# Bank alternation in the up projection and a 512 + 32 column split in the output projection of a decoder layer on one NeuronCore

## The chip, the cores and the metric

The kernel runs on one core of one Trainium2 chip. The metric is the device time of that core in microseconds. Before the change the median of two runs is 2403.22 us (2402.18 and 2404.27).

## The reference

One decoder layer serves a prompt of 512 tokens and 32 sample tokens (8 sequences with 4 new tokens each), all in float32, with a model width of 2048, 16 query heads, 4 key and value heads of 128, and a hidden width of 8192:

```python
xp, xs = rms_norm(hp, attn_norm), rms_norm(hs, attn_norm)
qp, kp, vp = project_qkv(xp, w_qkv, q_norm, k_norm)       # the same for the sample tokens
lf = log_sigmoid(x @ w_fgate + b_fgate); c = cumsum(lf)   # forgetting gates
mix_p = fox_attention(qp, kp, vp, c_p, c_p, 0, 128)
mix_s = fox_attention(qs, k_all, v_all, ...)              # 1024 cached keys from pages, and 4 new
hp, hs = hp + mix_p @ w_o, hs + mix_s @ w_o
h = h + square(relu(rms_norm(h, mlp_norm) @ w_up)) @ w_down
```

The outputs are the new activations, keys, values and log forget values of both groups.

## The kernel before, in words

Activations lie with the model dimension on the partitions and the tokens along the row: T = 544 columns (512 of the prompt, then 32 sample tokens), in 16 slices of 128 rows. `xT` is the residual stream. `act_hi` and `act_lo` hold the input of the current projection, split into two float32r parts whose sum is the float32 value. Every weight is split in the same way, and a product is computed as three matmuls: w_hi times the low part, w_hi times the high part and w_lo times the high part.

The weights go through the kernel in 338 units of 8 x 128 x 128 values (512 KB). For every unit SyncE loads `w_raw` (four buffers), ScalarE casts it into `w_hi` (L628, two buffers), VectorE subtracts to make `w_lo` (L906, two buffers), and TensorE multiplies. `unit` (L1323) is this last step: after a wait for w_lo it goes through the unit's 8 chunks, and a chunk is six matmuls, since the 544 columns are taken as two halves of HALF = 272. The accumulator is two banks of PSUM, half 0 in the first and half 1 in the second, 272 columns used of each:

```python
def acc(slot, rows=P):
    return ps[0:rows, 2 * slot:2 * slot + 2, 0:HALF]
```

Within a chunk the order is: half 0 by L1332 and L1333 (the same bank twice), half 1 by L1332 and L1333 (the other bank twice), then L1336 for half 0 and for half 1. Every matmul brings a weight load of its own, also where the weights are the ones just used. Two accumulators (slots 0 and 1, banks 0 to 3) are used in turn. An output tile of the query, key, value, output and up projections is two units (16 chunks, the whole model dimension); one of the down projection is one unit, and it is added to `xT` for each of 8 blocks of the hidden width.

The stages follow each other on TensorE: transposes of the input, gates, values, keys and queries (50 units, `model_tile`), the prompt's attention, the sample tokens' attention, the output projection (32 units, 16 tiles, `model_tile`), and 8 blocks of the MLP, each with 16 units of up projection (`up_tiles`) and 16 of down projection (`down_tiles`), the last with the transposes of the output among them.

Around the output projection: VectorE adds each tile's accumulator to `xT` (L1236) and frees the slot (`acc_free`), ScalarE squares the row (L834) and GpSimd adds the squares for the next norm. Around an up tile: VectorE takes the accumulator through relu and the norm's factor (L1260), ScalarE squares it and makes `u_hi`, VectorE makes `u_lo`. The order of everything is written out by hand in one program for each engine, with semaphores between them. TensorE's waits in these stages are for w_lo, for a free slot, and at a stage's first tile for the chunks of its input.

Of the kernel before, what the change touches and what calls it, by code (L numbers as in the profile page):

```python
# [31 lines left out]
ALU = mybir.AluOpType  # L32
# [6 lines left out]
def fox_layer(nc, x_prompt, x_sample, cache_k, cache_v, cache_logf, page_table, attn_norm, w_qkv, q_norm,  # L39
              k_norm, w_fgate, b_fgate, w_o, mlp_norm, w_up, w_down,  # L40
              y_prompt, y_sample, nk_prompt, nv_prompt, nf_prompt, nk_sample, nv_sample, nf_sample):
    _, SEQ, D = x_prompt.shape
    NB, DS, _ = x_sample.shape
    _, NPOOL, PAGE, NKV, HD = cache_k.shape
    NH = cache_logf.shape[3]
    NPG = page_table.shape[1]
# [3 lines left out]
    T = SEQ + NS  # L50
    HALF = T // 2
# [3 lines left out]
    UC = 8  # L55
# [11 lines left out]
    with ExitStack() as ctx:  # L67
        def sem(name):
            return ctx.enter_context(nc.semaphore(name))
# [5 lines left out]
        def at(name, shape, dt, offset=None):  # L75
            n = 4
            for s in shape[1:]:
                n *= s
            if offset is None:
                offset = top[0]  # L80
                top[0] += -(-n // 64) * 64
            return nc.alloc_sbuf_tensor_at(name, shape, dt, offset=offset), offset, offset + n

        xT, _, _ = at("xT", [P, KC, T], F32)
        act_hi, act_at, _ = at("act_hi", [P, KC, T], F32R)
        act_lo, _, act_end = at("act_lo", [P, KC, T], F32R)
# [3 lines left out]
        w_hi, _, _ = at("w_hi", [P, 2, UC, P], F32R)  # L90
        w_lo, _, _ = at("w_lo", [P, 2, UC, P], F32R)
# [85 lines left out]
        psf = ps[:, :, :].rearrange("p b n -> p (b n)")  # L177
# [5 lines left out]
        def halves(ap):  # L183
            return ap.rearrange("p (a n) -> p a n", a=2)

        def acc(slot, rows=P):
            return ps[0:rows, 2 * slot:2 * slot + 2, 0:HALF]
# [20 lines left out]
        w_lo_made = sem("w_lo_made")  # L208
        unit_used = sem("unit_used")
        acc_free = [sem("acc_free0"), sem("acc_free1")]  # L210
# [63 lines left out]
        mix_lo = sem("mix_lo")  # L274
# [11 lines left out]
        BLK_U, BLK_T = 32, 24  # L286
# [615 lines left out]
        def _(dve):  # L902
# [306 lines left out]
            last = (NB // 2 - 1, 1)  # L1209
# [15 lines left out]
            def o_tile(i, k):  # L1225
                u, t = U_O + 2 * k, T_O + k
                split(i + (u + 2) // 4, (u + 2) % 4)
                split(i + (u + 3) // 4, (u + 3) % 4)
                o_add(i, k)

            def o_add(i, k):
                u, t = U_O + 2 * k, T_O + k
                dve.wait_ge(unit_used, 4 * i + u + 2)
                dst = xT[:, 2 * i + k, :] if isinstance(i, int) else \
                    xT[:, bass.ds(2 * i + k, 1), :].rearrange("p o t -> p (o t)")
                nc.vector.tensor_tensor(halves(dst), halves(dst), acc(t % 2), ALU.add).then_inc(acc_free[t % 2], 1)  # L1236

            o_tile(0, 0)
            o_tile(0, 1)
# [5 lines left out]
            for c in range(KC):  # L1245
                gained_lo(1, g_mlp, c)
                if c == 1:
                    o_add(KC // 2 - 1, 1)
                    split((U_M + 1) // 4, (U_M + 1) % 4)
# [52 lines left out]
        def _(pe):  # L1302
# [4 lines left out]
            for c in range(KC):  # L1307
# [4 lines left out]
                for t, (t0, n) in enumerate(token_tiles):  # L1312
                    o = 2048 + 1024 * (c % 2) + t0
                    ins = pe.transpose(psf[:, o:o + n], x_tok[0:n, t, c * P:(c + 1) * P], ident[0:n, 0:n])
                ins.then_inc(x_turned, 1)

            def column_sums(src, out, signal):

                for a in range(2):
                    ins = pe.matmul(out[:, a, :], ones[:], src[:, a * HALF:(a + 1) * HALF], start=True, stop=True)  # L1320
                ins.then_inc(signal, 1)

            def unit(i, k, out, hi, lo, first, last, chunk_waits=None):  # L1323

                pe.wait_ge(w_lo_made, 4 * i + k + 1)
                s = k % 2
                for c in range(UC):
                    if chunk_waits is not None:
                        chunk_waits(c)
                    for a in range(2):  # L1330
                        h, l = hi(c)[:, a * HALF:(a + 1) * HALF], lo(c)[:, a * HALF:(a + 1) * HALF]
                        pe.matmul(out[:, a, :], w_hi[:, s, c, :], l, start=first and c == 0, stop=False)  # L1332
                        pe.matmul(out[:, a, :], w_hi[:, s, c, :], h, start=False, stop=False)  # L1333
                    for a in range(2):
                        h = hi(c)[:, a * HALF:(a + 1) * HALF]
                        ins = pe.matmul(out[:, a, :], w_lo[:, s, c, :], h, start=False, stop=last and c == UC - 1)  # L1336
                ins.then_inc(unit_used, 1)
                return ins

            def model_tile(i, u, t, waits=None, between=None, wait_acc=True):  # L1340

                if wait_acc:
                    pe.wait_ge(acc_free[t % 2], i + t // 2)
                out = acc(t % 2)
                for half in range(2):
                    uu = u + half
                    unit(i + uu // 4, uu % 4, out, lambda c: act_hi[:, half * UC + c, :],
                         lambda c: act_lo[:, half * UC + c, :], half == 0, half == 1,
                         None if waits is None else (lambda c: waits(half * UC + c)))
                    if half == 0 and between is not None:  # L1350
                        between()

            def norm_waits(n):
                def waits(c):
                    pe.wait_ge(act_lo_made, KC * n + c + 1)
                return waits


            model_tile(0, 0, 0, waits=norm_waits(0), wait_acc=False)
            pe.wait_ge(sq_added, KC - 1)  # L1360
            column_sums(tmp_c[:, 0, :], acc(2), ssq_ready)
# [12 lines left out]
            for i in range(NKV // 2):  # L1374
                for k in range(2):
                    u, t = U_V + 2 * k, T_V + k
                    model_tile(i, u, t, wait_acc=not (i == 0 and k == 0), between=turn_gates if 2 * i + k == 1 else None)
# [13 lines left out]
            def kq_tile(i, k, u0, t0, m0):  # L1391
                u, t, m = u0 + 2 * k, t0 + k, m0 + k
                first = isinstance(i, int) and m + 2 * i == 0
                model_tile(i, u, t, between=None if first else (lambda: head_sums(i, m - 1)))
# [9 lines left out]
            for b in range(NB):  # L1404
                ins = pe.matmul(psf[:, 3072 + b * PAGE:3072 + (b + 1) * PAGE],
                                lf_page[:, b * NPG:(b + 1) * NPG, :].rearrange("p n h -> p (n h)"), tri[:],
                                start=True, stop=True)
# [172 lines left out]
            last = (NB // 2 - 1, 1)  # L1580
# [5 lines left out]

            for k in range(2):
                u, t = U_O + 2 * k, T_O + k
                model_tile(0, u, t, waits=(lambda c: pe.wait_ge(mix_lo, c + 1)) if k == 0 else None)
            with pe.Fori(1, KC // 2) as i:  # L1590
                for k in range(2):
                    u, t = U_O + 2 * k, T_O + k
                    model_tile(i, u, t)

            def up_tiles(j, i, waits=None):
                for k in range(2):
                    u, t = U_M + 2 * k, T_M + k
                    pe.wait_ge(acc_free[t % 2], j * (BLK_T // 2) + i + t // 2)
                    for half in range(2):
                        uu = u + half  # L1600
                        unit(j * (BLK_U // 4) + i + uu // 4, uu % 4, acc(t % 2),
                             lambda c: act_hi[:, half * UC + c, :], lambda c: act_lo[:, half * UC + c, :],
                             half == 0, half == 1,
                             None if waits is None or k else (lambda c: waits(half * UC + c)))
                        if waits is not None and k == 0 and half == 0:
                            pe.wait_ge(sq_added, 2 * (KC - 1))
                            column_sums(tmp_c[:, 0, :], acc(2), ssq_ready)
# [69 lines left out]
```

## Time and profile before

| what | value |
|---|---|
| median of the runs | 2403.22 us |
| the runs | 2402.18 and 2404.27 us |
| span of the profiled execution, from its first to its last instruction | 2395.7 us |
| TensorE busy in matmuls | 2289.5 us, 96% |
| VectorE, ScalarE, GpSimd busy | 945.3, 668.9, 164.8 us |
| mean granted TensorE clock | 0.986 |
| output projection, its first matmul to its last | 629.6 to 825.0 us of the span |
| matmuls in it | 1536 |
| units of up projection in the 8 MLP blocks | 128 (6144 matmuls) |

The page gives no time for the profiled execution besides its span. The faster of the two runs is 6.5 us longer than the span, the median 7.5 us: what lies around the program's instructions. A matmul's duration in the rows includes the way through the array and overlaps the next matmul, so the rate of a stretch is read from the distance between starts, or from the number of matmuls in a window without idle time.

### The profile page before, as it was taken

The page shows a single profiled execution, that of the slowest core. Times are in us where ns is not written, and L with a number is a line of the kernel's source. Part 1 is how long each engine was busy: PE and PEld are TensorE (multiplying, and loading weights), DVE is VectorE, ACT ScalarE, POOL GpSimd, SP SyncE. Part 2 cuts the span into 40 slices and gives each one's busy share as a digit, 9 for nine tenths or more (in the row PEclk, how much of TensorE's full clock was granted, in tenths as well). Part 3 has the DMA queues.
Part 4 walks back from the last instruction along what each step waited for, and adds up shares of the span by engine and source line. Part 5 has one row for each costly group of instructions (what it writes and reads, how often), then busy time and mean ns, then how long its engine had stood idle before and what let it go on. Part 6 is the DMA issues. An engine that isn't in the chain of part 4 may idle for free.

```text
span 2395.7 us, 44612 instructions
## 1 busy us (share of the span) xinstructions
PE 2289.5 (96%) x18061; PEld 2212.0 (92%) x18061; DVE 945.3 (39%) x1188; ACT 668.9 (28%) x938; POOL 164.8 (7%) x245
## 2 busy tenths in 40 slices
PE   6999996777899999999999999999999999999998
PEld 5999994545799999999999999999999999999998
DVE  6366668944422443333333323323333333333332
ACT  4233336632322332122122112212212212212212
POOL 5400002233011100000000000000000000000000
PEclk9999998989899999999999999999999999999999
DMA  4333222179333233332323233333322233333333
GB/s 131 87 90 88 84 75 72 35 230 300 113 88 88 79 88 89 88 88 85 87 85 87 86 88 88 88 88 88 87 85 86 85 87 87 88 88 88 88 88 92
DMA packets 392889, 229.27 MB, mean 96 GB/s; under 512 B 18736, under 2 KB 372528, under 8 KB 392832
## 3 DMA queue, kind: packets, MB, share of 16 engines
q1 hardware_dynamic: 385376, 216.91, 31.1%
q0 software_dynamic: 7456, 11.55, 1.6%
q8 instruction: 42, 0.69, 0.1%
q14 instruction: 15, 0.12, 0.0%
HBM read 221.14 MB, written 7.28 MB: 95 GB/s over the span
## 4 chain that ended last, share of the span: by engine, by line
PE 87%; DVE 4%; DMA 2%; ACT 2%; issue 2%; SPq 2%; POOL 1%; ACTq 0%; DVEq 0%; POOLq 0%
PE ps L1333 28%; PE ps L1332 28%; PE ps L1336 28%; DMA k_high<-in_cache_k 2%; DVE probs L1074 1%; PE ps L1542 1%; POOL tmp_c L525 1%; DVE probs L1076 1%; ACT w_hi L628 1%; DVE nmax L1080 0%; ACT probs L720 0%; PE ps L1465 0%; PE ps L1504 0%; PE ps L1440 0%; SPq L410 0%
## 5 line engine op out<-in xcount | busy, mean ns | idle before, releaser
L1332 PE MATMUL ps<-act_lo,w_hi 128*128 128x272 f32 x3360 | 910.7, 289 | 7.8 <-DVE act_lo L917 3.9
L1333 PE MATMUL ps<-act_hi,w_hi 128*128 128x272 f32 x3360 | 909.6, 290 | 0.0
L906 DVE TENSOR_TENSOR w_lo<-w_raw,w_hi 128x1024 fp32r<-128x1024 f32 x338 | 415.3, 1229 | 1177.7 <-ACT w_hi L628 1177.5
L628 ACT CAST w_hi<-w_raw 128x1024 fp32r<-128x1024 f32 x338 | 354.3, 1048 | 1333.0 <-PE ps L1336 1333.0
L1336 PE MATMUL ps<-act_hi,w_lo 128*128 128x272 f32 x3360 | 698.5, 289 | 0.0
L1332 PEld LDWEIGHTS ps<-act_lo,w_hi 128*128 128x128 f32 x3360 | 634.8, 189 | 8.9 <-issue 4.1
L1333 PEld LDWEIGHTS ps<-act_hi,w_hi 128*128 128x128 f32 x3360 | 636.2, 189 | 0.1
L1332 PE MATMUL ps<-u_lo,w_hi 128*128 128x272 f32 x2048 | 554.4, 289 | 1.1
L1333 PE MATMUL ps<-u_hi,w_hi 128*128 128x272 f32 x2048 | 553.2, 289 | 0.0
L1336 PEld LDWEIGHTS ps<-act_hi,w_lo 128*128 128x128 f32 x3360 | 527.4, 189 | 0.0
L1336 PE MATMUL ps<-u_hi,w_lo 128*128 128x272 f32 x2048 | 425.0, 289 | 0.0
L1332 PEld LDWEIGHTS ps<-u_lo,w_hi 128*128 128x128 f32 x2048 | 385.8, 188 | 2.8 <-DVE u_lo L1264 2.8
L1333 PEld LDWEIGHTS ps<-u_hi,w_hi 128*128 128x128 f32 x2048 | 386.4, 189 | 0.0
L1336 PEld LDWEIGHTS ps<-u_hi,w_lo 128*128 128x128 f32 x2048 | 320.5, 188 | 0.0
L1284 DVE TENSOR_TENSOR xT<-xT,ps 128x544 f32 (+1 forms) x128 | 91.3, 713 | 13.2 <-PE ps L1336 13.2
L1264 DVE TENSOR_TENSOR u_lo<-tmp_b,u_hi 128x544 f32 (+1 forms) x64 | 46.4, 726 | 104.4 <-ACT u_hi L864 104.4
L862 ACT ACTIVATE tmp_b<-tmp_a 128x544 f32<-128x544 f32 x64 | 42.1, 658 | 126.8 <-DVE tmp_a L1260 126.8
L1017 DVE RECIPROCAL tmp_c<-tmp_c 128x544 f32<-128x544 f32 x20 | 70.9, 3546 | 0.8 <-ACT tmp_c L676 0.8
L525 POOL TENSOR_TENSOR tmp_c<-tmp_c,tmp_b 128x544 f32<-128x544 f32 x30 | 45.0, 1499 | 209.8 <-ACT tmp_b L834 207.4
L1454 PEld LDWEIGHTS ps<-ident,probs 128*128 128x128 f32 x160 | 19.8, 154 | 40.9 <-DVE probs L1089 28.0
L1454 PE MATMUL ps<-ident,probs 128*128 128x128 f32 x160 | 23.6, 302 | 29.7 <-DVE pT L1098 26.9
L729 ACT ACTIVATE probs<-probs,nmax 128x128 f32<-128x128 f32 (+1 forms) x64 | 36.0, 569 | 41.8 <-DVE nmax L1080 41.7
(163 smaller groups left out, 1147.5 us busy)
## 6 DMA issues: line engine op xcount, KB each, us to landing
w_raw<-in_w_up SPq DMA_DIRECT2D x128, 512.0 KB, 4.0
w_raw<-in_w_down SPq DMA_DIRECT2D x128, 512.0 KB, 3.9
w_raw<-in_w_qkv SPq DMA_DIRECT2D x48, 512.0 KB, 3.7
w_raw<-in_w_o SPq DMA_DIRECT2D x32, 512.0 KB, 3.9
k_low<-in_cache_k SPq DMA_DIRECT2D x32, 256.0 KB, 4.4
k_high<-in_cache_k SPq DMA_DIRECT2D x32, 256.0 KB, 5.2
v_page<-in_cache_v SPq DMA_DIRECT2D x32, 256.0 KB, 6.3
v_page<-in_cache_v POOLq DMA_DIRECT2D x32, 256.0 KB, 6.0
```

Source lines behind the costliest of these rows:

```text
L525: nc.gpsimd.tensor_tensor(tmp_c[:, 0, :], tmp_c[:, 0, :], tmp_b[:, c % 2, :], ALU.add).then_inc(sq_added, 1)
L628: nc.scalar.copy(w_hi[:, k % 2], w_raw[:, k % 4]).then_inc(w_hi_made, 1)
L729: nc.scalar.activation(probs[:, k, t, 0:w], probs[:, k, t, 0:w], ACT.Exp, bias=nmax[:, k % 2, t:t + 1], accum_out=rsum[:, k % 2, t:t + 1]) ...
L862: nc.scalar.activation(tmp_b[:, k, :], tmp_a[:, k, :], ACT.Square).then_inc(relu_sq, 1)
L906: nc.vector.tensor_tensor(w_lo[:, k % 2], w_raw[:, k % 4], w_hi[:, k % 2], ALU.subtract).then_inc(w_lo_made, 1)
L1017: nc.vector.reciprocal(tmp_c[:, 0, :], tmp_c[:, 0, :]).then_inc(head_rec, 1)
L1264: nc.vector.tensor_tensor(sl(u_lo), tmp_b[:, k, :], sl(u_hi), ALU.subtract).then_inc(u_lo_made, 1)
L1284: nc.vector.tensor_tensor(halves(dst), halves(dst), acc(t % 2), ALU.add).then_inc(acc_free[t % 2], 1)
L1332: pe.matmul(out[:, a, :], w_hi[:, s, c, :], l, start=first and c == 0, stop=False)
L1333: pe.matmul(out[:, a, :], w_hi[:, s, c, :], h, start=False, stop=False)
L1336: ins = pe.matmul(out[:, a, :], w_lo[:, s, c, :], h, start=False, stop=last and c == UC - 1)
L1454: ins = pe.transpose(psf[:, o:o + P], probs[:, k, t, j * P:(j + 1) * P], ident[:])
```

## The change

In `up_tiles` the unit's matmuls are put in another order: low part for half 0 and half 1, high part for half 0 and half 1, then the w_lo product for both. The number and the size of the matmuls stay. In the output projection a new `mixer_tile` calls `unit_split`, which cuts the 544 columns at 512 instead of 272: three matmuls of 512 columns, then three of 32. The accumulator there is one run of 544 columns from the slot's first bank, so 512 lie in that bank and 32 in the next, and VectorE's addition reads it in one run. Waits and semaphore counts are the same.

```diff
@@ o_add @@
-                nc.vector.tensor_tensor(halves(dst), halves(dst), acc(t % 2), ALU.add).then_inc(acc_free[t % 2], 1)
+                nc.vector.tensor_tensor(dst, dst, psf[:, 1024 * (t % 2):1024 * (t % 2) + T], ALU.add
+                                        ).then_inc(acc_free[t % 2], 1)
@@ tensor @@
+            def unit_turns(i, k, out, hi, lo, first, last, chunk_waits=None):
+
+                pe.wait_ge(w_lo_made, 4 * i + k + 1)
+                s = k % 2
+                for c in range(UC):
+                    if chunk_waits is not None:
+                        chunk_waits(c)
+                    for a in range(2):
+                        pe.matmul(out[:, a, :], w_hi[:, s, c, :], lo(c)[:, a * HALF:(a + 1) * HALF],
+                                  start=first and c == 0, stop=False)
+                    for a in range(2):
+                        pe.matmul(out[:, a, :], w_hi[:, s, c, :], hi(c)[:, a * HALF:(a + 1) * HALF],
+                                  start=False, stop=False)
+                    for a in range(2):
+                        ins = pe.matmul(out[:, a, :], w_lo[:, s, c, :], hi(c)[:, a * HALF:(a + 1) * HALF],
+                                        start=False, stop=last and c == UC - 1)
+                ins.then_inc(unit_used, 1)
+                return ins
+
+            def unit_split(i, k, out, hi, lo, first, last, chunk_waits=None):
+
+                pe.wait_ge(w_lo_made, 4 * i + k + 1)
+                s = k % 2
+                for c in range(UC):
+                    if chunk_waits is not None:
+                        chunk_waits(c)
+                    for cols in (slice(0, SEQ), slice(SEQ, T)):
+                        pe.matmul(out[:, cols], w_hi[:, s, c, :], lo(c)[:, cols], start=first and c == 0, stop=False)
+                        pe.matmul(out[:, cols], w_hi[:, s, c, :], hi(c)[:, cols], start=False, stop=False)
+                        ins = pe.matmul(out[:, cols], w_lo[:, s, c, :], hi(c)[:, cols], start=False,
+                                        stop=last and c == UC - 1)
+                ins.then_inc(unit_used, 1)
+                return ins
@@ after model_tile @@
+            def mixer_tile(i, u, t, waits=None):
+
+                pe.wait_ge(acc_free[t % 2], i + t // 2)
+                for half in range(2):
+                    uu = u + half
+                    unit_split(i + uu // 4, uu % 4, psf[:, 1024 * (t % 2):1024 * (t % 2) + T],
+                               lambda c: act_hi[:, half * UC + c, :], lambda c: act_lo[:, half * UC + c, :],
+                               half == 0, half == 1, None if waits is None else (lambda c: waits(half * UC + c)))
@@ output projection @@
-                model_tile(0, u, t, waits=(lambda c: pe.wait_ge(mix_lo, c + 1)) if k == 0 else None)
+                mixer_tile(0, u, t, waits=(lambda c: pe.wait_ge(mix_lo, c + 1)) if k == 0 else None)
...
-                    model_tile(i, u, t)
+                    mixer_tile(i, u, t)
@@ up_tiles @@
-                        unit(j * (BLK_U // 4) + i + uu // 4, uu % 4, acc(t % 2),
+                        unit_turns(j * (BLK_U // 4) + i + uu // 4, uu % 4, acc(t % 2),
```

TensorE in the output projection, one chunk before (`act_lo` and `act_hi` are the split input, `w_hi` and `w_lo` the split weights, `ps` is PSUM):

```order
L1332 MATMUL ps<-act_lo,w_hi 128x272
L1333 MATMUL ps<-act_hi,w_hi 128x272
L1332 MATMUL ps<-act_lo,w_hi 128x272
L1333 MATMUL ps<-act_hi,w_hi 128x272
L1336 MATMUL ps<-act_hi,w_lo 128x272 x2
```

and the same chunk of the changed kernel:

```order
L1368 MATMUL ps<-act_lo,w_hi 128x512
L1369 MATMUL ps<-act_hi,w_hi 128x512
L1370 MATMUL ps<-act_hi,w_lo 128x512
L1368 MATMUL ps<-act_lo,w_hi 128x32
L1369 MATMUL ps<-act_hi,w_hi 128x32
L1370 MATMUL ps<-act_hi,w_lo 128x32
```

Six matmuls and six weight loads stand there as before, with 1632 columns in all as before; three of the matmuls are now longer and three short, and the short ones stand in a row.

TensorE in the up projection reads before as in the first fence (the same lines of `unit`). The chunk of the changed kernel there:

```order
L1349 MATMUL ps<-act_lo,w_hi 128x272 x2
L1352 MATMUL ps<-act_hi,w_hi 128x272 x2
L1355 MATMUL ps<-act_hi,w_lo 128x272 x2
```

Each x2 is half 0 and then half 1, so every matmul now goes to the other bank than the one ahead of it. On the other engines no instruction moves.

## Rows read from the trace of the kernel before

**Rows 1.** The page: TensorE's busy time, and its granted clock in 40 slices.

```profile
PE 2289.5 (96%) x18061; PEld 2212.0 (92%) x18061; DVE 945.3 (39%) x1188; ACT 668.9 (28%) x938; POOL 164.8 (7%) x245
...
PEclk9999998989899999999999999999999999999999
```

**Rows 2.** Busy time in two stretches: the output projection, and its steady part.

```profile
core 0: us, PE busy (x) PEld busy (x) DVE busy (x) ACT busy (x) POOL busy (x), PEclk, DMA share, GB/s
629.00:825.00 196.00, 195.38 (x1536) 195.19 (x1536) 57.46 (x62) 50.34 (x61) 18.98 (x14) 0.99 0.29 83
640.00:820.00 180.00, 180.00 (x1436) 180.00 (x1435) 45.59 (x45) 41.23 (x45) 18.98 (x14) 1.00 0.31 88
```

**Rows 3.** Groups by line, 640 to 820 us: busy, mean ns, idle and releaser.

```profile
L1333 PE MATMUL ps<-act_hi,w_hi 128*128 128x272 f32 x479 | 129.4, 290 | 0.0
...
L1332 PEld LDWEIGHTS ps<-act_lo,w_hi 128*128 128x128 f32 x478 | 90.0, 188 | 0.0
...
L906 DVE TENSOR_TENSOR w_lo<-w_raw,w_hi 128x1024 fp32r<-128x1024 f32 x30 | 36.8, 1225 | 130.8 <-ACT w_hi L628 130.8
L628 ACT CAST w_hi<-w_raw 128x1024 fp32r<-128x1024 f32 x30 | 31.5, 1049 | 108.4 <-PE ps L1336 108.4
...
L1236 DVE TENSOR_TENSOR xT<-xT,ps 128x544 f32 (+1 forms) x15 | 10.7, 713 | 0.0
```

**Rows 4.** Timeline of TensorE, 700.5 to 702.9 us: start, duration, instruction.

```profile
700.54 0.29 PE L1332 MATMUL ps<-act_lo,w_hi 128*128 128x272 f32 x1
700.67 0.29 PE L1333 MATMUL ps<-act_hi,w_hi 128*128 128x272 f32 x1
700.79 0.29 PE L1332 MATMUL ps<-act_lo,w_hi 128*128 128x272 f32 x1
700.92 0.29 PE L1333 MATMUL ps<-act_hi,w_hi 128*128 128x272 f32 x1
701.04 0.41 PE L1336 MATMUL ps<-act_hi,w_lo 128*128 128x272 f32 x2
701.29 0.29 PE L1332 MATMUL ps<-act_lo,w_hi 128*128 128x272 f32 x1
...
702.80 0.29 PE L1332 MATMUL ps<-act_lo,w_hi 128*128 128x272 f32 x1
```

**Rows 5.** The same view near the stage's start, at half clock.

```profile
632.48 0.43 PE L1332 MATMUL ps<-act_lo,w_hi 128*128 128x272 f32 x1
...
633.84 0.43 PE L1332 MATMUL ps<-act_lo,w_hi 128*128 128x272 f32 x1
```

**Rows 6.** Timeline around two 8-column matmuls, weight loads (PEld) among them.

```profile
206.19 0.31 PEld L1413 LDWEIGHTS ps<-c_pg,earlier 128*128 128x128 f32 x2
206.31 0.28 PE L1413 MATMUL ps<-c_pg,earlier 128*128 128x8 f32 x2
206.42 0.19 PEld L1332 LDWEIGHTS ps<-act_lo,w_hi 128*128 128x128 f32 x1
206.45 0.37 PE L1332 MATMUL ps<-act_lo,w_hi 128*128 128x272 f32 x1
206.53 0.19 PEld L1333 LDWEIGHTS ps<-act_hi,w_hi 128*128 128x128 f32 x1
206.66 0.29 PE L1333 MATMUL ps<-act_hi,w_hi 128*128 128x272 f32 x1
206.66 0.19 PEld L1332 LDWEIGHTS ps<-act_lo,w_hi 128*128 128x128 f32 x1
```

**Rows 7.** Timeline of TensorE around one head's product of probabilities and values.

```profile
490.82 2.32 PE L1465 MATMUL ps<-pT,v_st 128*128 128x512 f32 x8
492.98 0.71 PE L1454 MATMUL ps<-ident,probs 128*128 128x128 f32 x5
```

**Rows 8.** One line's instructions: counts, durations in ns, shapes.

```profile
L1465 PE MATMUL ps<-pT,v_st x128: 272/485/1062, 396.3 to 499.3; 128*128 128x512 f32 x32, 128*128 128x384 f32 x32, 128*128 128x256 f32 x32, 128*128 128x128 f32 x32
```

## The prediction

> **What bounds the kernel now.** I read the page first, for which engine is full. TensorE is busy for 2289.5 of 2395.7 us and no other engine passes 40% of the span [rows 1]. The clock line shows 9 (90% or more) outside three slices, so the columns run at 2.4 GHz nearly everywhere. Then the windows of the output projection, the stage of the larger edit: between 640 and 820 us TensorE is busy for 180.00 of 180 us with 1436 matmuls, at a granted clock of 1.00 [rows 2]. So there a matmul starts every 180/1436 = 0.1253 us, and nothing waits. The reader is to see beside it what the others do: in the same 180 us VectorE makes w_lo 30 times (36.8 us) and waits 130.8 us for ScalarE, ScalarE casts 30 times (31.5 us) and waits 108.4 us for TensorE, and the addition L1236 takes 10.7 us [rows 3]. The weights are ready early. Whatever a chunk of six matmuls costs on TensorE goes straight into the time, one for one.
>
> Third, the timeline, for the step between two starts. From 700.54 to 702.80 there are three chunks, 0.753 us each, 0.1256 us a matmul [rows 4]. At 2.4 GHz 272 columns take 0.1133 us, so 12 ns come on top. The same matmul at half clock, near the stage's start, shows no such excess: six take 633.84 - 632.48 = 1.36 us, 0.2267 each, which is 272 columns at 1.2 GHz and nothing more [rows 5]. So the 12 ns belong to something that doesn't halve with the clock, and the weight load that every matmul brings is the candidate.
>
> **What a weight load costs.** The trace has one place where the matmuls are too short to cover it. Two 8-column matmuls are followed by the next unit, and there the weight loads start at 206.42 and 206.53, 0.11 us apart, while one of them covers a matmul of 8 columns and the next waits behind it: the matmul of 206.45 is recorded with 0.37 us instead of 0.29, since it was issued and then held up for 0.08 us [rows 6]. The next load, 0.13 us later, runs beside 272 columns. So a load is hidden behind a matmul that lasts over 0.11 us, and where the matmul is shorter the load sets the step, at 0.11 to 0.13 us.
>
> The Trainium skill, page "TensorE: Matmul & The Clock Gate", section "LDWEIGHTS (loading the stationary operand)", says that a load takes its column count over 1.2 GHz, whatever the rows. For 128 columns that is an estimate of 107 ns from that page, and the trace agrees with its 0.11 us. The sum doesn't use it.
>
> **The output projection.** Its 1536 matmuls are 768 pairs. A pair is now 2 x 0.1253 = 0.2507 us. After the change a pair is one matmul of 512 columns and one of 32.
>
> - 512 columns at 2.4 GHz are 0.2133 us, long enough to cover the next load. What comes on top has no row, since no full-rate stream of that width is in the trace. From below: the plain float32 matmuls of L1465, which take two clocks a column and show as two records each, have eight records of 512, 512, 384, 384, 256, 256, 128 and 128 columns between 490.82 and 492.98 [rows 7, 8]. That is 2.16 us for 2560 columns, 2.133 us at two clocks each, so 3 ns a record: 0.216 us. From above: the excess grows with the columns as it stands at 272, 0.1256 x 512/272 = 0.236 us. With the 12 ns kept per matmul it is 0.226. I take 0.222, between the first and the last.
> - 32 columns are 13 ns of work, and the step is the load of the matmul behind it. A run of three short ones has three such steps (32 to 32 twice, then 32 to the next 512). From below 0.11 us, from above the 0.125 of now. I take 0.113, since the array's stream is nearly idle beside these loads, as it was at 206.42 [rows 6].
>
> A pair becomes 0.222 + 0.113 = 0.335 us, which is 0.084 more, and 768 pairs give +64.7 us. The ends: 0.216 + 0.11 = 0.326 gives +57.8; 0.236 + 0.125 = 0.361 gives +84.7. The stage grows from 195.4 to some 260 us.
>
> Nothing hides it. ScalarE and VectorE need 1.05 and 1.23 us for a unit that now takes 6.0 us and will take 8.0 [rows 3], and the final tile's addition is the same 0.71 us; read in one run over two banks instead of two, it carries the same 544 columns, and I cost it at nothing. Even 0.1 us on each of 16 additions would lie under the next tile but for the last. The next norm's squares, on GpSimd, get more time per tile, not less. The stage's first microseconds run at half clock [rows 5]; there a pair would go from 0.453 to 0.427 + 0.11 us, the same 0.084.
>
> **The up projection.** 128 units of 8 chunks, 6144 matmuls, whose count, columns and loads stay. The diff is in the banks: of the six steps of a chunk, two stay in a bank now (L1332 to L1333, twice) and four change it; afterwards all six change. So the trace of before shows the price of both. The steps within a bank read 0.13 and 0.13, those that change it 0.12, 0.12 and a mean of 0.125 over two [rows 4]; starts are given to 10 ns, and over three chunks all six have a mean of 0.1256. I see no difference, and with one of up to 5 ns either way on two steps of each of 1024 chunks the bound is -10 to +10 us. I take 0. What the alternation would relieve, a matmul that waits for the one ahead to leave its bank, would have shown in these two steps.
>
> **The sum.** 2395.7 + 64.7 + 0 = 2460.4 us of span. The median of the runs stands 7.5 us above the span of before (2403.2 against 2395.7), so 2468 us, 2.7% more. A difference under about 2% (48 us) can't be told from none by a measurement of this kernel: the bounds of slower lie at 2451.
>
> **The rivals.**
>
> *The short matmuls cost next to nothing (7%).* If the load of a matmul could run ahead by more than one, three short ones would be covered by the 512-column ones, which leave 0.1 us of the load path free each. For it: the two 8-column matmuls are recorded within 0.28 us, the second 28 ns behind the first [rows 6]. Against: the loads themselves keep their 0.11 us, and the matmul behind is held up. A pair would be 0.222 + 0.028 = 0.250, the change 768 x 0 = 0, and the time 2403, not slower. It decides as soon as a short matmul takes less than 0.09 us (then the total is under 2%).
> The skill's page "TensorE: Matmul & The Clock Gate", section "Wait — 56ns, not 53.3ns?", speaks for this one: it gives N/2.4 plus 2.5 ns for a warm matmul and a floor of about 25 ns for small ones, 216 + 25 = 241 ns for the pair by that page, an estimate of 2396 us. It is a rule for matmuls without loads of their own, and rows 6 show the load.
>
> *The alternation does pay (5%).* If the 12 ns were a collision in PSUM that only a full alternation avoids, the 6144 matmuls would fall to 0.1133 + 0.003 = 0.1163 us, 9 ns each, -57 us, and the total would be 2468 - 57 = 2411: no change. Against: four of six steps alternate already and are no faster [rows 4].
>
> *A narrow matmul in this format runs as two records (5%),* as the plain float32 ones do [rows 8], with two loads each: 0.222 + 0.226 = 0.448 a pair, +151 us, 2555.
>
> *The clock drops in the output projection (3%).* The array streams 544 columns, 227 ns, in 335 ns instead of in 251, and the page shows 8 tenths in slices of the attention [rows 1]. At half clock throughout a pair is 0.427 + 0.11, +220 us, 2623; a tenth of the stage so costs some 20 us more.
>
> **How the numbers follow.** The forecast as worked out has 80%: 2468, with an own range from 2403.2 + 57.8 - 10 = 2451 to 2403.2 + 84.7 + 10 = 2498. The ends of both terms together are unlikely, and the rivals lie on both sides of it, so the range is 2450 to 2496. Slower by over 2% holds 76 of the 80, with the two dear rivals 84%. Within 2%: 4 of the forecast, and most of the first two rivals, 14%. Faster by over 2% needs both of these together, 2%.
>
> **What would show it.** In the output projection's timeline of the changed kernel the three 512-column starts should lie 0.216 to 0.236 us apart and the three short ones 0.11 to 0.125; the window of that stage should hold the same 1536 matmuls in about 260 us with no idle time and a clock of 1.00. In the up projection the mean step should still read 0.125 or 0.126, and a block of the MLP should take the same time. The forecast is wrong if the short steps read under 0.09, if the wide ones show another excess than 3 to 23 ns, if the up projection's step moves by over 2 ns, or if TensorE idles in the output projection for something else.

## The result, and the profile after

The changed kernel takes 2473.97 us (median of 2 runs, 2473.61 and 2474.32) against 2403.22 us: 1.0307 times as long, with a 95% interval of 1.0285 to 1.0329. The forecast was 2468 us, in a range from 2450 to 2496.

The span went from 2395.7 to 2472.7 us, 77.0 more. By the page of the changed kernel TensorE alone is busy for longer, 2362.1 us instead of 2289.5, while the other engines' work is the same to 0.3 us. These lines answer to [rows 1]:

```profile
PE 2362.1 (96%) x18061; PEld 2249.3 (91%) x18061; DVE 945.6 (38%) x1188; ACT 668.7 (27%) x938; POOL 164.8 (7%) x245
...
PEclk9999998988899999999999999999999999999999
```

The windows of the output projection, as in [rows 2], over the whole stage and its steady part:

```profile
core 0: us, PE busy (x) PEld busy (x) DVE busy (x) ACT busy (x) POOL busy (x), PEclk, DMA share, GB/s
637.00:904.00 267.00, 266.46 (x1536) 232.56 (x1536) 57.02 (x62) 50.19 (x61) 18.91 (x14) 0.99 0.21 61
650.00:900.00 250.00, 250.00 (x1458) 218.39 (x1458) 46.82 (x46) 41.32 (x45) 18.91 (x14) 1.00 0.22 64
```

The same 1536 matmuls fill 266.5 us instead of 195.4, without idle time, and at full clock but for the first 5.7 us. In the steady part that is 2 x 250/1458 = 0.343 us a pair, against 0.251.

One chunk and a little more in the timeline of weight loads (PEld) and matmuls; the columns are start, duration and instruction:

```profile
699.84 0.40 PE L1369 MATMUL ps<-act_hi,w_hi 128*128 128x512 f32 x1
699.84 0.19 PEld L1370 LDWEIGHTS ps<-act_hi,w_lo 128*128 128x128 f32 x1
700.07 0.39 PE L1370 MATMUL ps<-act_hi,w_lo 128*128 128x512 f32 x1
700.07 0.19 PEld L1368 LDWEIGHTS ps<-act_lo,w_hi 128*128 128x128 f32 x1
...
700.30 0.18 PE L1368 MATMUL ps<-act_lo,w_hi 128*128 128x32 f32 x1
700.30 0.19 PEld L1369 LDWEIGHTS ps<-act_hi,w_hi 128*128 128x128 f32 x1
700.33 0.26 PE L1369 MATMUL ps<-act_hi,w_hi 128*128 128x32 f32 x1
700.41 0.19 PEld L1370 LDWEIGHTS ps<-act_hi,w_lo 128*128 128x128 f32 x1
700.44 0.26 PE L1370 MATMUL ps<-act_hi,w_lo 128*128 128x32 f32 x1
700.52 0.19 PEld L1368 LDWEIGHTS ps<-act_lo,w_hi 128*128 128x128 f32 x1
700.55 0.48 PE L1368 MATMUL ps<-act_lo,w_hi 128*128 128x512 f32 x1
700.63 0.19 PEld L1369 LDWEIGHTS ps<-act_hi,w_hi 128*128 128x128 f32 x1
700.87 0.40 PE L1369 MATMUL ps<-act_hi,w_hi 128*128 128x512 f32 x1
```

Two things are to be read here. From the first short matmul on, the loads start at 700.30, 700.41, 700.52 and 700.63: 0.11 us each, one behind the other. They set the pace and the array waits. And the matmuls' own starts mislead in this place. The second short one starts 0.03 us behind the first, but has 0.26 us instead of 0.18; the wide one at 700.55 has 0.48 instead of 0.40, and its successor comes 0.32 us later. A start is the moment at which a matmul was let go, and the 0.08 us on top of its duration are its wait for the weights. Add them, and the steps are 0.23, 0.11, 0.11, 0.11. It is the pattern of the 8-column matmuls in [rows 6].

At half clock, in the stage's first microseconds, the timeline of TensorE reads:

```profile
637.17 0.77 PE L1368 MATMUL ps<-act_lo,w_hi 128*128 128x512 f32 x1 [1.85 <-DVE act_lo L1221]
...
639.08 0.77 PE L1368 MATMUL ps<-act_lo,w_hi 128*128 128x512 f32 x1
639.65 0.63 PE L1369 MATMUL ps<-act_hi,w_hi 128*128 128x512 f32 x1
640.08 0.63 PE L1370 MATMUL ps<-act_hi,w_lo 128*128 128x512 f32 x1
...
641.00 0.77 PE L1368 MATMUL ps<-act_lo,w_hi 128*128 128x512 f32 x1
```

A chunk takes 1.92 us: three times 0.427 for the wide ones, and 0.213 for each short one. So the load takes twice as long at half the clock.

For the up projection the chain that ended last gives a mark once a block, ScalarE's cast of the same unit. First the kernel before, then the changed one:

```profile
1894.09 1.06 ACT w_hi L628
...
2087.34 1.06 ACT w_hi L628
...
2280.59 1.06 ACT w_hi L628
```

```profile
1391.89 1.06 ACT w_hi L628
...
1584.94 1.06 ACT w_hi L628
...
1777.99 1.06 ACT w_hi L628
```

A block takes 193.25 us before and 193.05 after. Now and then a block has 0.4 or 0.8 us more than that (one of the seven between these marks before, three of the seven after), in both kernels; such blocks are left out of the comparison. The new order gives 0.2 us for 16 units of 48 matmuls, which is 0.27 ns a matmul, and 1.6 us for the 128 units.

The stage's 71.1 us less these 1.6 leave 7.5 of the 77.0 us, and they lie ahead of the output projection. Its first matmul starts at 637.17 us, where the kernel before has it at 629.62 us. No edit stands there. The stage before it waits for pages of the cache (TensorE's waits for `k_high` sum to 19.2 us before and 24.8 after), and its length varies from run to run: in the kernels below the first matmul comes between 629.98 and 635.36 us. It is the reason too why the medians differ by 70.8 us and these two spans by 77.0. The profiled execution of the kernel before was a short one: in each later run the time is 1.6 us above the run's own span (2474.32 and 2472.7 us here), so that execution took some 2397 us and is neither of the two timed ones. The 6.5 and 7.5 us that the table of before puts down to what lies around the instructions are for the most part this difference between executions.

### The profile page after: what moved, and what is told of

It is laid out like the page before. It is cut to its first block, busy times and chain, and to the rows that moved or that the text cites. A ratio compares the mean times of both kernels' runs of the same rounds, so it can differ in the third digit from the quotient of the medians.

```text
span 2472.7 us, 44612 instructions
## 1 busy us (share of the span) xinstructions
PE 2362.1 (96%) x18061; PEld 2249.3 (91%) x18061; DVE 945.6 (38%) x1188; ACT 668.7 (27%) x938; POOL 164.8 (7%) x245
## 4 chain that ended last, share of the span: by engine, by line
PE 88%; DVE 3%; SPq 2%; DMA 2%; ACT 2%; issue 2%; POOL 1%; ACTq 0%; DVEq 0%; POOLq 0%
PE ps L1333 14%; PE ps L1334 14%; PE ps L1337 14%; PE ps L1355 10%; PE ps L1349 10%; PE ps L1352 10%; PE ps L1368 4%; PE ps L1369 4%; PE ps L1370 4%; DMA k_high<-in_cache_k 2%; PE ps L1509 1%; PE ps L1586 1%; DVE probs L1074 1%; POOL tmp_c L525 1%; SPq L410 1%
## 5 line engine op out<-in xcount | busy, mean ns | idle before, releaser
L1349 PE MATMUL ps<-act_lo,w_hi 128*128 128x272 f32 x2048 | 424.4, 288 | 2.5 <-DVE act_lo L917 2.5
L1355 PE MATMUL ps<-act_hi,w_lo 128*128 128x272 f32 x2048 | 424.4, 289 | 0.0
L1352 PE MATMUL ps<-act_hi,w_hi 128*128 128x272 f32 x2048 | 422.8, 288 | 0.0
L1349 PEld LDWEIGHTS ps<-act_lo,w_hi 128*128 128x128 f32 x2048 | 322.5, 188 | 3.2 <-issue 1.8
L1352 PEld LDWEIGHTS ps<-act_hi,w_hi 128*128 128x128 f32 x2048 | 322.3, 189 | 0.0
L1355 PEld LDWEIGHTS ps<-act_hi,w_lo 128*128 128x128 f32 x2048 | 320.2, 189 | 0.0
L1333 PE MATMUL ps<-act_lo,w_hi 128*128 128x272 f32 x800 | 217.6, 290 | 2.1 <-DVE w_lo L906 2.1
L1334 PE MATMUL ps<-act_hi,w_hi 128*128 128x272 f32 x800 | 217.0, 290 | 0.0
L1368 PE MATMUL ps<-act_lo,w_hi 128*128 128x512 f32 (+1 forms) x512 | 169.2, 330 | 1.8 <-DVE act_lo L1221 1.8
L1369 PE MATMUL ps<-act_hi,w_hi 128*128 128x512 f32 (+1 forms) x512 | 169.1, 330 | 0.0
L1337 PE MATMUL ps<-act_hi,w_lo 128*128 128x272 f32 x800 | 166.5, 289 | 0.0
L1370 PE MATMUL ps<-act_hi,w_lo 128*128 128x512 f32 (+1 forms) x512 | 163.1, 330 | 0.0
L1333 PEld LDWEIGHTS ps<-act_lo,w_hi 128*128 128x128 f32 x800 | 151.6, 189 | 2.3 <-DVE w_lo L906 2.2
L1334 PEld LDWEIGHTS ps<-act_hi,w_hi 128*128 128x128 f32 x800 | 151.9, 190 | 0.0
```

The lines of the kernel that those rows point to most:

```text
L1349: pe.matmul(out[:, a, :], w_hi[:, s, c, :], lo(c)[:, a * HALF:(a + 1) * HALF], start=first and c == 0, stop=False)
L1352: pe.matmul(out[:, a, :], w_hi[:, s, c, :], hi(c)[:, a * HALF:(a + 1) * HALF], start=False, stop=False)
L1355: ins = pe.matmul(out[:, a, :], w_lo[:, s, c, :], hi(c)[:, a * HALF:(a + 1) * HALF], start=False, stop=last and c == UC - 1)
L1368: pe.matmul(out[:, cols], w_hi[:, s, c, :], lo(c)[:, cols], start=first and c == 0, stop=False)
L1369: pe.matmul(out[:, cols], w_hi[:, s, c, :], hi(c)[:, cols], start=False, stop=False)
L1370: ins = pe.matmul(out[:, cols], w_lo[:, s, c, :], hi(c)[:, cols], start=False, stop=last and c == UC - 1)
```

## The experiments

**Each half of the change alone.** The first kernel keeps `unit_turns` and gives the output projection its `model_tile` back:

```diff
-                mixer_tile(0, u, t, waits=(lambda c: pe.wait_ge(mix_lo, c + 1)) if k == 0 else None)
+                model_tile(0, u, t, waits=(lambda c: pe.wait_ge(mix_lo, c + 1)) if k == 0 else None)
```

(the loop's call and `o_add` likewise). Expected:

> The bank alternation in the up projection alone, the output projection as before. Theory (a bank change costs nothing and gives nothing): within 0.2% of the kernel before, 2401 to 2405 us, and an MLP block takes 193.0 to 193.3 us as before and after. Rival (the alternation itself helps): the spans of the changed kernel show blocks 0.2 us shorter, so 1.6 us less in all, and the ratio would lie at 0.999; rival (it costs): over 1.001.

Measured: 2396.46 us (12 runs), ratio 0.999, interval 0.9976 to 1.0003; blocks of 193.05 us. The first rival's number came out, and the theory that nothing happens holds only as far as the total can tell: the gain is in every block of the trace, and too small for these runs to tell from none.

The second keeps the cut and gives the up projection its old order:

```diff
-                        unit_turns(j * (BLK_U // 4) + i + uu // 4, uu % 4, acc(t % 2),
+                        unit(j * (BLK_U // 4) + i + uu // 4, uu % 4, acc(t % 2),
```

> The 512 + 32 cut in the output projection alone, the up projection as before. Theory: the whole loss is here, 71 us over the kernel before (2474 us, ratio 1.029 to 1.031), the stage's chunk at 1.035 us. Rival (part of the loss is from elsewhere, the attention stage that ran 7 us longer in the changed kernel's profile): under 1.027, with 64 us in the stage.

Measured: 2473.39 us, ratio 1.0315, interval 1.029 to 1.0341. The whole loss is the cut. Its steady window, 650 to 895 us, has 1429 matmuls in 245.00 us, 0.343 us a pair.

**Wide and short in turn.** The chunk's six matmuls in another order:

```diff
-                    for cols in (slice(0, SEQ), slice(SEQ, T)):
-                        pe.matmul(out[:, cols], w_hi[:, s, c, :], lo(c)[:, cols], ...)
-                        pe.matmul(out[:, cols], w_hi[:, s, c, :], hi(c)[:, cols], ...)
-                        ins = pe.matmul(out[:, cols], w_lo[:, s, c, :], hi(c)[:, cols], ...)
+                    for cols in both:
+                        pe.matmul(out[:, cols], w_hi[:, s, c, :], lo(c)[:, cols], ...)
+                    for cols in both:
+                        pe.matmul(out[:, cols], w_hi[:, s, c, :], hi(c)[:, cols], ...)
+                    for cols in both:
+                        ins = pe.matmul(out[:, cols], w_lo[:, s, c, :], hi(c)[:, cols], ...)
```

> The changed kernel with the cut's matmuls in the order wide, short, wide, short, wide, short. Theory (a load can run ahead of one matmul only, so each short one exposes the next load, wherever it stands): chunk still 1.03 to 1.04 us, time equal to the changed kernel within 3 us. Rival (short matmuls wait since they follow each other onto the same 32 columns of PSUM): the two short-to-short waits go, 0.08 us each, chunk about 0.87 us, 41 us less than the changed kernel. Rival (loads queue up two deep): the short ones vanish, chunk about 0.80 us.

Measured: 2692.85 us, ratio 1.1227 (1.12 to 1.1254), in all four runs within 3 us. None of the three had this. Its windows over the stage show why:

```profile
640.00:1120.00 480.00, 480.00 (x1501) 407.55 (x1501) 47.47 (x46) 42.21 (x46) 18.78 (x14) 0.50 0.12 34
```

The granted clock is 0.50 from 0.6 us into the stage to its end. Its first rows show where it fell, the row of a wide and a short one going from 0.48 to 0.80 us:

```profile
629.98 0.48 PE L1369 MATMUL ps<-act_lo,w_hi 128*128 128x512 f32 x2 [1.84 <-DVE act_lo L1221]
...
630.72 0.80 PE L1373 MATMUL ps<-act_hi,w_lo 128*128 128x512 f32 x2
```

Every kernel here runs its first microseconds of this stage at half clock, behind the small matmuls and waits of the sample tokens' attention. The others came back to full clock 3.5 to 5.8 us into the stage, and with this order it never rose. A pair takes 2 x 480/1501 = 0.640 us, which is 0.427 + 0.213, the same as for the changed kernel's order at that clock. So the question of the run was answered at half clock (a short matmul exposes one load in either order), but the time came from something else, and the same was to be asked at full clock.

**The same from a full clock.** The first two tiles take `model_tile` (and their additions the old form), the other 14 the interleaved order:

```diff
-                mixer_tile(0, u, t, waits=(lambda c: pe.wait_ge(mix_lo, c + 1)) if k == 0 else None)
+                model_tile(0, u, t, waits=(lambda c: pe.wait_ge(mix_lo, c + 1)) if k == 0 else None)
```

> The order wide, short, wide, short, ... again, but the output projection's first two tiles go as 272 twice, so that the clock is at full rate when it begins (in the run before, it stayed at half for the whole stage: chunk 1.92 us, its short ones still exposing a load each, 0.213 us). Theory A (the interleaved order keeps a clock that is up): chunk 1.035 us as in the changed kernel, total 2472 to 2476 us, since a short matmul exposes one load in either order. Rival (short ones after each other wait on PSUM): 0.87 us. Theory B (this order also brings the clock down): 30 of 32 units at 1.92 us a chunk, 2680 us.

Measured: 2460.02 us, ratio 1.0244 (1.0217 to 1.0271). Its windows, the first two tiles with the start of the third, and the rest; and its timeline, in which a wide and a short one are merged into a row (x2):

```profile
635.00:660.00 25.00, 24.64 (x184) 24.67 (x185) 13.97 (x20) 11.49 (x19) 0.00 (x0) 0.93 0.18 52
662.00:890.00 228.00, 228.00 (x1325) 198.53 (x1324) 43.15 (x42) 37.91 (x42) 18.80 (x14) 1.00 0.22 64
```

```profile
700.25 0.50 PE L1372 MATMUL ps<-act_lo,w_hi 128*128 128x512 f32 x2
700.60 0.49 PE L1374 MATMUL ps<-act_hi,w_hi 128*128 128x512 f32 x2
700.94 0.49 PE L1376 MATMUL ps<-act_hi,w_lo 128*128 128x512 f32 x2
701.28 0.50 PE L1372 MATMUL ps<-act_lo,w_hi 128*128 128x512 f32 x2
```

The clock stays at 1.00 and a chunk takes 1.03 us, as theory A had it. The total lies 12 us under the lower end that I gave, 9 of which I had forgotten: the two tiles in halves save 32 chunks of 0.28 us. The other 3 are within the 8 us by which its two runs differ. So the exposed load comes from the short matmul alone and not from the one before it in the same columns, and no load ran two matmuls ahead. And the same order of instructions runs at either clock for hundreds of microseconds. What differs is what TensorE did before: here 26 us of 272-column matmuls without a pause, the last 22 of them at full clock, and in the run before a wait of 1.84 us. At what point between these two it would tip wasn't tried.

**The short ones taken away.** The 32 columns are left out (in VectorE's addition too), so that the sample tokens get no output projection:

```diff
-                    for cols in (slice(0, SEQ), slice(SEQ, T)):
+                    for cols in (slice(0, SEQ),):
```

> The changed kernel without the 32-column matmuls in the output projection (the sample tokens' part of that projection is left out). It takes the suspected cost away. Theory (three wide steps of 0.233 us, and each short one adds an exposed load of 0.112): chunk 0.698 us, 256 chunks fall by 86 us, stage about 180 us, total some 2387 us, or 15 under the kernel before. Rival (the wide steps are dear because short ones with their late loads stand beside them): the wide steps fall too, to 0.216, and the total to 2374.

Measured: 2382.72 us, ratio 0.9923 (0.9904 to 0.9943). Its steady window:

```profile
650.00:810.00 160.00, 160.00 (x691) 129.20 (x690) 43.91 (x43) 39.82 (x43) 19.06 (x14) 1.00 0.33 94
```

160/691 = 0.2316 us for a wide step. In the changed kernel's timeline the wide steps that no wait distorts read 0.23 us too (700.07 to 700.30). Alone or beside short ones a wide one costs the same, so a short one costs 0.343 - 0.2316 = 0.111 us: the load. For 6% of the columns that is a third of the pair.

**Other cuts.** Each part in its own bank, 384 + 160 columns in even tiles and 304 + 240 in odd ones:

```diff
+        CUTS = [384, 304]
...
-                    for cols in (slice(0, SEQ), slice(SEQ, T)):
+                    for b, cols in enumerate((slice(0, w), slice(w, T))):
+                        o = out[:, b, 0:cols.stop - cols.start]
```

(and two additions in `o_add`). Expected:

> The changed kernel with the 544 columns cut at 384 in even tiles (384 + 160) and at 304 in odd ones (304 + 240), two additions on VectorE a tile. From the changed kernel's trace a full-rate step of N columns is about 4 ns + 0.447 ns x N (272: 0.1256 us, 512: 0.2327 us) and no step is under the load's 0.112. Theory: 384 at 0.176 and 160 at 0.112 us, 304 at 0.140 and 240 at 0.112; stage 207 us, total some 14 us over the kernel before. Rival (12 ns a matmul beside 2.4 GHz where a load runs beside it, and the wide one's excess is something else): 384 at 0.172, 304 at 0.139, 240 at 0.112 too. The two differ at 384 by 4 ns; a pair of 304 + 240 costs as much as 272 twice by both.

Measured: 2412.27 us, ratio 1.0053 (1.0033 to 1.0073). Its timeline, at the seam of two tiles and a chunk later:

```profile
699.89 0.34 PE L1373 MATMUL ps<-act_hi,w_hi 128*128 128x384 f32 x1
700.07 0.34 PE L1374 MATMUL ps<-act_hi,w_lo 128*128 128x384 f32 x1
700.24 0.24 PE L1372 MATMUL ps<-act_lo,w_hi 128*128 128x160 f32 x1
...
701.33 0.30 PE L1372 MATMUL ps<-act_lo,w_hi 128*128 128x304 f32 x1
701.47 0.30 PE L1373 MATMUL ps<-act_hi,w_hi 128*128 128x304 f32 x1
701.61 0.30 PE L1374 MATMUL ps<-act_hi,w_lo 128*128 128x304 f32 x1
701.74 0.28 PE L1372 MATMUL ps<-act_lo,w_hi 128*128 128x240 f32 x1
701.86 0.28 PE L1373 MATMUL ps<-act_hi,w_hi 128*128 128x240 f32 x1
701.97 0.28 PE L1374 MATMUL ps<-act_hi,w_lo 128*128 128x240 f32 x1
702.08 0.30 PE L1372 MATMUL ps<-act_lo,w_hi 128*128 128x304 f32 x1
```

384 columns take 0.175 us, 304 take 0.139, and both 240 and 160 are at the load's 0.11. A chunk of 304 + 240 is 0.75 us, no more than 272 twice. So between 240 and 304 columns the place of the cut is free, and past that each column moved over costs. The total is 11 us over the kernel before, where 14 were expected; half of the tiles lose 0.036 us a pair, 14 us of the stage by the steps, less the 1.6 us of the up projection, and the rest is within what the runs of the kernel before vary (2390 to 2405 us).

**Where the wide step's excess comes from.** It was the term of the sum that I had under its size. PSUM first, with every matmul starting anew (the sum over chunks and parts is left out):

```diff
-                        pe.matmul(out[:, cols], w_hi[:, s, c, :], lo(c)[:, cols], start=first and c == 0, stop=False)
+                        pe.matmul(out[:, cols], w_hi[:, s, c, :], lo(c)[:, cols], start=True, stop=True)
```

> The changed kernel with every matmul of the output projection starting anew in PSUM instead of adding (its sum over chunks and parts is left out). If the read and add in PSUM costs the 19 ns of a wide step: 0.216 us, chunk 0.985 us, total some 13 us less than the changed kernel. If not: 0.233 us and 1.035 us, the same total. If the short ones wait for the sum ahead of them in the same 32 columns, their 0.112 falls too.

Measured: 2469.26 us, ratio 1.0282 (1.0259 to 1.0306). The window from 650 to 895 us has the same 1429 matmuls in 245.00 us as with the sum, so accumulating costs nothing, for wide and short ones; the total is 5 us under the changed kernel's, of which 2.8 are a stage that starts earlier. Then the operands' format, bfloat16 in this projection alone (a constant tile of ones stands for the weights, so its result is left out):

```diff
-                        pe.matmul(out[:, cols], w_hi[:, s, c, :], lo(c)[:, cols], start=first and c == 0, stop=False)
+                        pe.matmul(o, ones_b[:], lo(c)[:, c0:c1], start=first and c == 0, stop=False)
```

> The changed kernel with bfloat16 operands in the output projection alone: its input split into two bfloat16 parts, and a constant tile of bfloat16 ones for every weight (so this projection's result is left out). It asks where the wide step's 19 ns beyond 512 columns at 2.4 GHz come from. If from the 4-byte stream or its weight load: wide steps at 0.216 us. If from the array or the write into PSUM: 0.233 us still. The short step shows the load of a 2-byte tile: 0.11 us if it goes by columns alone, less if by bytes. Chunk 0.98 to 1.04 us with loads at 0.112, near 0.8 with loads at half that.

Measured: 2390.12 us, ratio 0.9954 (0.9938 to 0.9971). Its timeline:

```profile
699.97 0.18 PE L1375 MATMUL ps<-b_lo,ones_b 128*128 128x32 bf16 x1
...
700.00 0.18 PE L1376 MATMUL ps<-b_hi,ones_b 128*128 128x32 bf16 x1
...
700.02 0.18 PE L1377 MATMUL ps<-b_hi,ones_b 128*128 128x32 bf16 x1
...
700.05 0.38 PE L1375 MATMUL ps<-b_lo,ones_b 128*128 128x512 bf16 x1
...
700.26 0.38 PE L1376 MATMUL ps<-b_hi,ones_b 128*128 128x512 bf16 x1
700.27 0.10 PEld L1377 LDWEIGHTS ps<-b_hi,ones_b 128*128 128x128 bf16 x1
```

Both terms go. The wide step is 0.215 us, 2 ns over its columns at 2.4 GHz, and the short one 0.025, its load out of sight. A chunk takes 0.72 us. Two halves of 272 in bfloat16 weren't run. With the same 2 ns over their columns they would take 0.69 us a chunk, an estimate from this run's wide step, so the cut at 512 is no gain with 2-byte operands either, but its loss shrinks from 0.28 us a chunk to about 0.03. So the load's 0.11 us and the column's extra time both go with the 4-byte format, as far as a run with weights that are all ones can show it. Whether the extra time is the format's own rate, or the moving columns and the load contending for a way in, these runs don't tell: every matmul here had a load beside it.

**The alternation everywhere.** Since its gain was in every block, `unit_turns` was put into all units of the kernel before:

```diff
-                    unit(i + uu // 4, uu % 4, out, lambda c: act_hi[:, half * UC + c, :],
+                    unit_turns(i + uu // 4, uu % 4, out, lambda c: act_hi[:, half * UC + c, :],
...
-                    unit(j * (BLK_U // 4) + i + u // 4, u % 4, acc(t % 2), lambda c: u_hi[:, c, :],
+                    unit_turns(j * (BLK_U // 4) + i + u // 4, u % 4, acc(t % 2), lambda c: u_hi[:, c, :],
```

> The kernel before with the alternating order in every unit of all projections, 272 columns twice everywhere. The changed kernel's blocks of up projection took 96.22 us against 96.43, 0.21 us for 16 units. Theory (the gain is by chunk, wherever it stands): 338 units give 4.4 us, ratio 0.998 to 0.999, and the down projection's 96.83 us a block falls to 96.6. Rival (the gain is an accident of the up projection's loop): down stays at 96.83 and the ratio at 0.999 or over.

Measured: 2392.42 us against 2401.01, ratio 0.9967, interval 0.9954 to 0.998. The interval lies wholly under 1, so it beats the kernel before, and with it the changed one. The marks of its blocks:

```profile
1509.75 1.06 ACT w_hi L628
...
1702.60 1.06 ACT w_hi L628
```

192.85 us a block: the down projection gains another 0.2. By such blocks that is 3.2 us in the MLP and some 4 in all, and the runs show 5 to 11 us. Part of the rest is in the trace too. No block here takes over 192.86 us, and one takes 192.42, while in each trace with `unit` in the down projection one to three of the seven blocks are 0.4 or 0.8 us longer than the usual one. The seven blocks take 1349.5 us here and 1353.6 before, so with the other stages the gain is some 5.7 us, an estimate from these two traces. Why the blocks of one trace differ isn't known.

The order changes two things at once, the bank at each step and which operand is read after which. The last kernel keeps the first and crosses the second:

```diff
-                    for a in range(2):
-                        pe.matmul(out[:, a, :], w_hi[:, s, c, :], lo(c)[:, a * HALF:(a + 1) * HALF], ...)
-                    for a in range(2):
-                        pe.matmul(out[:, a, :], w_hi[:, s, c, :], hi(c)[:, a * HALF:(a + 1) * HALF], ...)
+                    for n, (a, x) in enumerate(((0, lo), (1, hi), (0, hi), (1, lo))):
+                        pe.matmul(out[:, a, :], w_hi[:, s, c, :], x(c)[:, a * HALF:(a + 1) * HALF], ...)
```

> Banks alternate at each matmul of every projection, as in the run before (ratio 0.9967, blocks of 96.0 and 96.4 us), but the order within a chunk is low part for half 0, high part for half 1, high part for half 0, low part for half 1, then w_lo twice: every one of the first four steps also changes between act_lo and act_hi. Theory (the bank is what counts): blocks of 96.0 and 96.4 us and the ratio at 0.996 to 0.998 again. Rival (what helped is that two matmuls after each other read the same part): the blocks go back to 96.4 and 96.8 or over, the ratio to 1.000.

Measured: 2391.86 us against 2400.38, ratio 0.9961 (0.9944 to 0.9978), and its marks are again 192.87 and 192.85 us apart:

```profile
1893.10 1.07 ACT w_hi L628
...
2085.97 1.06 ACT w_hi L628
...
2278.82 1.06 ACT w_hi L628
```

The gain stays when the operands' order is crossed, so the repeated operand isn't the cause. What both orders share is that the half changes at each matmul, and with it two things: the bank that is written and the columns of the input that are read. No run changes one without the other, so that the bank is the cause is likely and not shown.

## Why the prediction was right, point by point

- **What bounds the stage.** Right. TensorE has no idle time in it before or after, and the loss of a pair came through one for one: 0.0922 us x 768 = 70.8 us, and the stage grew by 71.1. That the medians differ by exactly 70.8 is in part luck, since the up projection's 1.6 us are in them too and the runs of one kernel vary by more.
- **The short matmul at its load, 0.113 us.** Right: 0.111. The run without short ones, the interleaved order and the other cuts show it from three sides. The reading of [rows 6], that the second 8-column matmul's early start is no early finish, was the right one. The rival that short ones cost nothing is refuted for this format and holds for bfloat16, where the section "Wait — 56ns, not 53.3ns?" of "TensorE: Matmul & The Clock Gate" in the Trainium skill fits the rows well (0.215 and 0.025 us against its 215.7 and 25 ns). The bfloat16 matmuls had loads of their own, so the prediction's reason for setting the rule aside (that it is one for matmuls without loads) missed what decided: how long the load takes in this format.
- **The wide matmul, 0.222 us.** This is the term that was mis-sized: 0.2316. The 12 ns on top of 272 columns were put down to the load, as something that doesn't halve with the clock, and would stay as they are for any width. But the load does follow the clock (0.111 and 0.213 us), and the excess grows: 12 ns at 272 and 304 columns, 15 at 384, 18 at 512. The four steps lie on 5 ns plus 0.443 ns a column. The upper end of the bound, growth with the columns (0.236), was nearer than the value chosen. 0.0096 us on 768 pairs are 7.4 us. The short one was 0.002 us too dear, 1.5 us, and the up projection's 1.6 us went the same way; with the 1 us of the next point that leaves 5.3 of the 6 us by which the forecast fell short, and the rest is less than two runs can tell.
- **Half clock at the stage's start.** Its short step was put at 0.11 us there and is 0.213, so a pair is 0.640 us and not 0.537. On three chunks that is 1 us. It would have mattered in the rival of the fallen clock: 768 pairs at 0.640 us would add 299 us, not the 220 given.
- **The up projection, no change.** Right for the time, and wrong in the small: 0.2 us a block, 1.6 in all, where the rival that the alternation pays had 57. Starts given to 10 ns could not show it; a mark once a block could.
- **The fallen clock, 3%.** It didn't come for this order of the short matmuls, and came in full for the interleaved one. With the edit written that way the result would have been +12%.
- **Two records for a narrow matmul, 5%.** It didn't come: the stage has 1536 matmuls as before, and each short one has one load.
- **The same work elsewhere.** VectorE's addition over two banks in one run takes its 0.71 us as before, and nobody waited longer for it.

## What to carry to other kernels

With 4-byte operands and a load for each, a matmul of up to some 240 columns costs its weight load, 0.11 us, however few they are (32, 160 and 240 were measured): cut an odd number of columns into even parts, each over that width, not into a full one and a rest. With 2-byte operands the same cut costs next to nothing, so know the format before using a rule on small matmuls. Read a row's start together with its duration: a matmul that starts early and lasts longer than its kind is waiting.

## What the runs showed of the hardware that I had not expected

- One and the same order of matmuls (512 and 32 columns in turn) ran at half clock for a stage of 490 us when it came right behind the attention and a wait, and at full clock for 231 us when it came behind 22 us of matmuls at full clock. With the three wide ones first and the three short ones after them, the same matmuls rose from half clock at the stage's start in each of the three traces with that order. What in the pattern decides isn't settled.
- The weight load of a 4-byte tile follows the clock: 0.111 us at full, 0.213 at half. The Trainium skill's page "TensorE: Matmul & The Clock Gate", section "LDWEIGHTS (loading the stationary operand)", gives one figure for it, columns over 1.2 GHz; the trace of the 4-byte tile agrees at full clock alone.
- A 4-byte column costs more than its 0.417 ns at full clock (0.443 on top of 5 ns, from 272, 304, 384 and 512 columns), and exactly its 0.833 at half clock (0.427 us for 512).
- Going to the other half, and so to the other bank of PSUM, at each matmul takes 0.2 us off 16 units of 6 us, with the same count and sizes. It is so in each of the eight traces with that order in the up projection alone and in the two with it everywhere.
